# Root reciprocals spread by transposing broadcast columns, and two rescheduled norms of the mixer outputs, in a one-core fp32 encoder layer

## What is computed

```python
h = rms_norm(x, norm1_g) * (1 + sc1) + sh1         # norm 1, all 1024 positions
z = h @ w_in                                       # 19 units of 128 columns
ya, yb, yc, yd = gmlp(z), dsa(z), pool(z), swa(z)  # four mixers, 256 features each
y = _rms(stack([ya, yb, yc, yd])) * mix_out_g      # each mixer's 256 features by themselves
x = x + g1 * (y @ w_out)
h = rms_norm(x, norm2_g) * (1 + sc2) + sh2         # norm 2
x = x + g2 * conv_glu(h, w_up, conv, w_down)
out = rms_norm(x, final_g)                         # final norm
```

## Time and profile before

| | us |
|---|---|
| median of 3 runs | 1311.04 |
| the runs | 1307.82 to 1311.52 |
| the profiled execution, its own time | 1310.75 |
| its span, first to last instruction | 1309.0 |
| busy: PE, DVE, ACT, POOL | 1217.2, 718.3, 595.2, 630.1 |

### The profile page before, as it was taken

One profiled execution on the slowest core, in us unless ns is written; L12 is line 12 of the kernel. 1 busy time (PEld: TensorE's weight loads), 2 busy tenths in 40 slices (PEclk: granted clock), 3 DMA queues, 4 the chain that ended last, 5 costly groups with the idle time before them and its releaser, 6 DMA issues.

```text
span 1309.0 us, 16977 instructions
## 1 busy us (share of the span) xinstructions
PE 1217.2 (93%) x5618; PEld 995.1 (76%) x5618; DVE 718.3 (55%) x1404; ACT 595.2 (45%) x1007; POOL 630.1 (48%) x317
## 2 busy tenths in 40 slices
PE   3798999987899799999999999989799999999996
PEld 1686778866788588888878887878588888888874
DVE  6943877887857788889984444353522112211224
ACT  4236556654842455224422676542455224422442
POOL 1135576783304255445555566424255445544553
PEclk9999999987989799999999999999899999999998
DMA  8447753450112122242223443314222222222223
GB/s 311 147 178 261 203 171 110 146 165 17 49 65 96 50 97 97 94 133 97 97 95 130 132 137 128 130 57 139 76 98 97 93 99 95 99 94 95 97 100 128
DMA packets 58565, 153.87 MB, mean 118 GB/s; under 512 B 6504, under 2 KB 20200, under 8 KB 58512
## 3 DMA queue, kind: packets, MB, share of 16 engines
q1 hardware_dynamic: 47472, 135.12, 30.5%
q10 hardware_dynamic: 11040, 18.09, 4.2%
HBM read 142.66 MB, written 10.52 MB: 117 GB/s over the span
## 4 chain that ended last, share of the span: by engine, by line
PE 35%; issue 32%; POOL 16%; DVE 9%; DMA 3%; ACT 2%; ACTq 1%; POOLq 1%; SPq 0%; DVEq 0%
POOL w_lo L554 11%; PE ps L1779 8%; PE ps L1782 8%; PE ps L1780 8%; DVE unread L1282 4%; POOL act_lo L703 3%; PE ps L2058 2%; POOL w_ada L593 1%; PE ps L1760 1%; PE ps L1763 1%; PE ps L1761 1%; PE ps L2037 1%; PE ps L2047 1%; DMA w_ada<-in_w_ada 1%; DMA qi_dram<-qi_lo 1%
## 5 line engine op out<-in xcount | busy, mean ns | idle before, releaser
L554 POOL TENSOR_TENSOR w_lo<-w_raw,w_hi 128x1024 fp32r<-128x1024 f32 x152 | 364.6, 2399 | 487.5 <-ACT w_hi L715 487.5
L1779 PE MATMUL ps<-h_hi,w_hi 128*128 128x512 f32 x928 | 371.5, 400 | 11.6 <-DVE h_lo L1240 7.0
L1780 PE MATMUL ps<-h_lo,w_hi 128*128 128x512 f32 x928 | 364.3, 393 | 0.0
L1782 PE MATMUL ps<-h_hi,w_lo 128*128 128x512 f32 x928 | 345.6, 392 | 0.0
L715 ACT ACTIVATE w_hi<-w_raw 128x1024 fp32r<-128x1024 f32 x152 | 161.1, 1060 | 358.9 <-PE ps L1782 351.3
L1779 PEld LDWEIGHTS ps<-h_hi,w_hi 128*128 128x128 f32 x928 | 175.7, 189 | 56.7 <-DVE h_lo L1240 8.5
L1782 PEld LDWEIGHTS ps<-h_hi,w_lo 128*128 128x128 f32 x928 | 175.5, 189 | 37.6
L1780 PEld LDWEIGHTS ps<-h_lo,w_hi 128*128 128x128 f32 x928 | 176.3, 190 | 33.4
L1665 DVE SCALAR_TENSOR_TENSOR ps<-conv_in,conv_w,ps 128x512 f32<-128x512 f32 x44 | 33.2, 754 | 215.0 <-ACT ps L1090 215.0
L1779 PE MATMUL ps<-act_hi,w_hi 128*128 128x512 f32 x352 | 140.3, 398 | 5.0 <-POOL act_lo L703 2.6
L1782 PE MATMUL ps<-act_hi,w_lo 128*128 128x512 f32 x352 | 137.6, 391 | 0.0
(11 more groups left out here) (240 smaller groups left out, 1801.6 us busy)
## 6 DMA issues: line engine op xcount, KB each, us to landing
w_raw<-in_w SPq DMA_DIRECT2D x173, 512.0 KB, 3.3
w_ada<-in_w_ada SPq DMA_DIRECT2D x48, 512.0 KB, 4.2
x_sb<-in_x SPq DMA_DIRECT2D x4, 1024.0 KB, 9.9
q_st<-qk_dram SPq DMA_DIRECT2D x32, 128.0 KB, 4.1
out<-fin_o ACTq DMA_DIRECT2D x16, 256.0 KB, 2.1
qi_st<-qi_dram ACTq DMA_DIRECT2D x18, 128.0 KB, 3.6
qk_dram<-qk_hi ACTq DMA_DIRECT2D x4, 512.0 KB, 2.7
qk_dram<-qk_lo ACTq DMA_DIRECT2D x4, 512.0 KB, 3.7
```

Source lines behind the costliest of these rows:

```text
L554: pool.tensor_tensor(r(w_lo[:, slot]), w_raw[:, slot], w_hi[:, slot], ALU.subtract).then_inc(w_lo_ready, 1)
L1779: pe.matmul(ps[:, bank], r(hi_t[:, kk]), r(xh(kk)), start=(i == 0), stop=False)
L1780: pe.matmul(ps[:, bank], r(hi_t[:, kk]), r(xl(kk)), start=False, stop=False)
L1782: mm = pe.matmul(ps[:, bank], r(lo_t[:, kk]), r(xh(kk)), start=False, stop=last_k)
```

## The change

1. **Spread without diagonals.** `root` ends with the reciprocal. `spread` transposes, for each block, the column `root_r[:, t]` broadcast to 128 columns.
2. **gMLP squares on DVE.** In half 0 the four sums of squares of the gMLP rows are taken by DVE right behind `gmlp_output`; ACT no longer takes them. `y_roots` waits for them.
3. **Late squares one column up.** `late_squares(7)` and `y_roots` of half 1 move on ACT from k = 7 to k = 6, ahead of that step's `split_unit` and `square`.
4. **Late rows scaled in place.** In half 1 the rows of y are multiplied by their factor in SBUF, gMLP and pool on DVE (two instructions), SWA and DSA on ACT (eight), and PE transposes them; the diagonals of half 1 go.

```diff
-                squared = 16 * h
+                squared = 12 * h
...
+                def scale_late_rows(positions):
+
+                    act.wait_ge(y_inverted, 2)
+                    for m_ in positions:
+                        cols = slice(W * Y_GROUPS[m_], W * Y_GROUPS[m_] + W)
+                        for b in range(HB, NBLK):
+                            at_ = 4 * m_ + b - HB
+                            ins = act.activation(y[:, b, cols], y[:, b, cols], ACT.Copy, scale=y_scale[:, at_:at_ + 1])
+                        ins.then_inc(y_scaled_act, 1)
...
                         if k == NBLK + 1:
-                            y_roots(slice(0, 12), 15)
+                            act.wait_ge(gmlp_squared, HB)
+                            y_roots(slice(0, 12), 11)
...
                         if k == NBLK:
                             act.wait_ge(gmlp_out, 4)
-                            for b in range(HB):
-                                y_squares(b, (0,), junk)
                             act.wait_ge(swa_biased, NBLK)
...
+                            if k == 6:
+                                late_squares(NBLK - 1)
+                                y_roots(slice(0, 16), 28)
                             if k == 7:
-                                late_squares(NBLK - 1)
-                                y_roots(slice(0, 16), 32)
+                                scale_late_rows((2, 3))
                             split_unit(nd + k + 2)
...
-            def root(m, diag, blocks=HB):
+            def root(m, blocks=HB):
 
                 dve.wait_ge(root_ready, m + 1)
-                vlink(dve.reciprocal(root_r[:, 0:blocks], root_s[:, 0:blocks]))
-                dve.tensor_tensor(diag.rearrange("p (t c) -> p t c", c=P),
-                                  ident[:].unsqueeze(1).to_broadcast([P, blocks, P]),
-                                  root_r[:, 0:blocks].unsqueeze(2).to_broadcast([P, blocks, P]),
-                                  ALU.mult).then_inc(diag_ready, 1)
+                dve.reciprocal(root_r[:, 0:blocks], root_s[:, 0:blocks]).then_inc(root_inverted, 1)
...
+                def scale_late_rows(positions):
+                    dve.wait_ge(y_root_ready, 3)
+                    dve.reciprocal(y_scale[:], y_root[:]).then_inc(y_inverted, 2)
+                    dve.wait_ge(y_inverted, 2)
+                    for m_ in positions:
+                        rows = y[:, HB:NBLK, W * Y_GROUPS[m_]:W * Y_GROUPS[m_] + W]
+                        dve.tensor_tensor(rows, rows, y_scale[:, 4 * m_:4 * m_ + 4].unsqueeze(2).to_broadcast([P, HB, W]),
+                                          ALU.mult).then_inc(y_scaled, 1)
+
+                def gmlp_squares():
+                    dve.wait_ge(gmlp_out, 4)
+                    for b in range(HB):
+                        dve.scalar_tensor_tensor(out=gmlp_junk[:, b], in0=y[:, b, 0:W], scalar=1.0, in1=y[:, b, 0:W],
+                                                 op0=ALU.mult, op1=ALU.mult, accum_out=y_sum[:, b:b + 1]
+                                                 ).then_inc(gmlp_squared, 1)
...
                             for g in range(4):
                                 gmlp_output(g)
+                            gmlp_squares()
...
                         if k == 6:
-                            y_scales(1, range(4), 3)
+                            scale_late_rows((0, 1))
...
-            def spread(m, bank, diag, blocks=HB):
-
-                pe.wait_ge(diag_ready, m + 1)
-                for i in range(blocks // HB):
-                    mm = pe.matmul(ps[:, bank + i], ones[:], diag[:, HALF * i:HALF * i + HALF], start=True, stop=True)
-                mm.then_inc(rms_spread, 1)
+            def spread(m, bank, blocks=HB):
+
+                pe.wait_ge(root_inverted, m + 1)
+                for t in range(blocks):
+                    tr = pe.transpose(ps[:, bank + t // HB, P * (t % HB):P * (t % HB) + P],
+                                      root_r[:, t:t + 1].to_broadcast([P, P]), ident[:])
+                tr.then_inc(rms_spread, 1)
...
-                    pe.wait_ge(y_diag_ready, 4 * h + i // 2 + 1)
+                    if h == 0:
+                        pe.wait_ge(y_diag_ready, i // 2 + 1)
+                    elif i < 4:
+                        pe.wait_ge(y_scaled, i // 2 + 1)
+                    else:
+                        pe.wait_ge(y_scaled_act, i // 2 - 1)
...
-                        tr = pe.matmul(ps[:, Y_BANKS[h][i], P * t:P * t + P], y[:, HB * h + t, P * g:P * g + P],
-                                       diag_y_of[h][:, i // 2, t], start=True, stop=True)
+                        at_, rows = ps[:, Y_BANKS[h][i], P * t:P * t + P], y[:, HB * h + t, P * g:P * g + P]
+                        if h == 0:
+                            tr = pe.matmul(at_, rows, diag_y[:, i // 2, t], start=True, stop=True)
+                        else:
+                            tr = pe.transpose(at_, rows, ident[:])
```

More of the change, by code:

```diff
@@ L127, in build @@
         rms_x = at("rms_x", [P, S], RB + 12288)
-        diag_x = at("diag_x", [P, S], RB + 16384)
         h_t = at("h_t", [P, 2, S], RB)
@@ L155, in build @@
         p_t = at("p_t", [P, 2, HB, P], RE + 4096)
-        diag_y_of = [at("diag_y_0", [P, 4, HB, P], RB + 4096), at("diag_y_1", [P, 4, HB, P], RE)]
+        diag_y = at("diag_y", [P, 4, HB, P], RB + 4096)
+        gmlp_junk = at("gmlp_junk", [P, HB, W], RB + 12288)
         sum2 = at("sum2", [P, HALF], RB + 28672)
-        diag2 = at("diag2", [P, HALF], RB + 30720)
         onehot = at("onehot", [32, S + P], RG)
@@ L270, in build @@
         root_ready = sem("root_ready")
-        diag_ready = sem("diag_ready")
+        root_inverted = sem("root_inverted")
         rms_spread = sem("rms_spread")
@@ L345, in build @@
         y_diag_ready = sem("y_diag_ready")
+        y_inverted = sem("y_inverted")
+        y_scaled = sem("y_scaled")
+        y_scaled_act = sem("y_scaled_act")
+        gmlp_squared = sem("gmlp_squared")
         x2_loaded = sem("x2_loaded")
@@ L1042, in _ @@
                     dsa_squares(HB - 1)
-                    y_roots(slice(12, 16), 16)
+                    y_roots(slice(12, 16), 12)
                 n0, s0 = N1 + 16 * h, 2 * KD + 16 * h
@@ L1210, in _ @@
             ada_tile(0, 1)
-            root(0, diag_x[:], NBLK)
+            root(0, NBLK)
             ada_tile(1, 0)
@@ L1557, in early_out, with y_scales @@
                                       ALU.mult).then_inc(dsa_out_ready, 1)
-                def y_scales(hh, groups, roots):
+                def y_scales(groups, roots):
                     dve.wait_ge(y_root_ready, roots)
@@ L1563, in y_scales @@
                     for m_ in groups:
-                        dve.tensor_tensor(diag_y_of[hh][:, m_], ident[:].unsqueeze(1).to_broadcast([P, HB, P]),
+                        dve.tensor_tensor(diag_y[:, m_], ident[:].unsqueeze(1).to_broadcast([P, HB, P]),
                                           y_scale[:, 4 * m_:4 * m_ + 4].unsqueeze(2).to_broadcast([P, HB, P]),
                                           ALU.mult).then_inc(y_diag_ready, 1)
+                def scale_late_rows(positions):
[12 more added lines that the diff above has]
+                                                 ).then_inc(gmlp_squared, 1)
                 if h == 0:
@@ L1600, in _ @@
                                 gmlp_output(g)
+                            gmlp_squares()
                         if k == NBLK + 1:
-                            y_scales(0, range(3), 1)
-                    y_scales(0, range(3, 4), 2)
+                            y_scales(range(3), 1)
+                    y_scales(range(3, 4), 2)
                 n0, s0 = N1 + 16 * h, 2 * KD + 16 * h
@@ L1645, in _ @@
                 else:
-                    root(2, diag2[:])
+                    root(2)
                     vlink(dve.memset(sum2[:], 0.0))
@@ L1652, in _ @@
                         final_norm(0, g)
-                root(1 + 2 * h, diag2[:])
+                root(1 + 2 * h)
                 dve.wait_ge(rms_spread, 2 + 2 * h)
@@ L1708, in _ @@
                         if k == 6:
-                            y_scales(1, range(4), 3)
-            root(4, diag2[:])
+                            scale_late_rows((0, 1))
+            root(4)
             dve.wait_ge(rms_spread, 5)
@@ L1722, in _, with over_features @@
             pe.sem_inc(residual_added, 2)
-            def over_features(m, count, bank, sums, diag, blocks=HB):
+            def over_features(m, count, bank, sums, blocks=HB):
                 row_sums(count, bank, sums, blocks)
-                spread(m, bank, diag, blocks)
+                spread(m, bank, blocks)
             def row_sums(count, bank, sums, blocks=HB):
@@ L1747, in _ @@
             last.then_inc(bias_row_made, 1)
-            over_features(0, KD, 4, sum_x, diag_x, NBLK)
+            over_features(0, KD, 4, sum_x, NBLK)
             pe.wait_ge(bias_row_out, 1)
@@ L2022, in _ @@
```

(6 more changed lines are left out.)

## The result

The changed kernel took 1292.2 us (median of 4 runs, 1288.57 to 1293.01) beside 1309.43 for the kernel before (4 runs): a ratio of 0.9866, 95% interval 0.9835 to 0.9897. Measured twice more it was 0.9865 (0.9843 to 0.9887) and 0.9858 (0.9834 to 0.9883). The mean of the three, 0.9863, is 17.9 us. The forecast was 15.9 us and 1295.0. The direction, the places and most prices held. The gain was 1.3 us larger than forecast in the first measurement and 2 us over all three; most of the 2 us lie in one term, the turning of y in half 1. The time itself came out 2.8 us under 1295. Of these 1.3 us are the larger gain, and 1.3 us are the base, which the forecast took as 1310.75 and which was 1309.43 here.

A forecast was written before the change was run, and what follows sets the result against it. PE, busy 1217 of 1309 us, was taken as the bound, with gains only where it waits or runs at 1.2 GHz. 5.1 + 0.4 + 0.9 + 5.4 + 4.1 = 15.9 us off 1310.75 gives 1294.9, stated as 1295; range 1292 to 1302.

The forecast's parts named there:

- Norm 2 and last norm: Norm 2 of both halves and the last norm: PE starts sooner with four transposes, 1.7 us each, 5.1 for three.
- Slow broadcast columns: Rival for the norms: broadcast columns load slowly, so only the diagonals' time is won; 1298.2 us, chance 0.05.
- m = 2: Final norm of half 0, beside the first w_out unit: only PE's time counts, 0.4 us, bounds 0 and 0.5.
- Norm 1: First norm (m = 0): without the diagonal h_t starts sooner, limited by POOL's subtractions; 0.9 us, bounds 0 and 3.0.
- POOL is not in the way: Rival in norm 1: POOL does not hold DVE back, 2.1 us more gained, 1292.8 us; chance 0.07.
- Turning of half 0: Turning of y, half 0: passes start 3.4 us sooner, full clock saves 2.4, less 0.4 for delays: 5.4 us.
- clock falls all the same: Rival in the turning of y, half 0: PE's clock still drops, since its work there is small; 1297.4 us, chance 0.12.
- the early gain doesn't reach the end: Rival: the 5.4 us from half 0 is lost because the load of x or DVE's key search keeps pace; 1300.3, chance 0.08.
- Turning of half 1: Turning of y, half 1: earlier root and four transposes instead of eight passes start w_out 4.1 us sooner; bounds 1.0 and 5.0.
- The rule that speaks against this: Half 1's turning: the skill says transposes do not engage the full clock; then it is worth 1.0 us, time 1298.
- Clock stays down: Rival in half 1: the clock stays low behind the late transposes, w_out at 869.9, gain 1.0 us, 1298; chance 0.18.
- slower: Rival after half 1's turning: clock stays at 1.2 GHz deep into w_out, up to 38 us lost, 1333; chance 0.03.

## Why the prediction was right in most terms, and the step that failed

- **Norm 2 and last norm, 5.1.** Right: 1.68, 1.68 and 1.7 to 1.9. A column read 128 times loads like a stored one: four transposes took 1.11 us against 1.09 in the earlier trace rows, both at a granted clock of 0.50. *Slow broadcast columns* is refuted.
- **m = 2, 0.4.** Right, 0.3 to 0.4.
- **Norm 1, 0.9; measured 1.3 to h_t and 1.2 to PE.** The step "the product starts ahead of POOL, and POOL waits for it" was drawn right; POOL's two then took 4.80 us from 27.41, ending at 32.2 and not 32.5, and the reciprocal to h_t shrank accordingly. The prediction misreads one row on the way: of POOL's two subtractions in the earlier trace rows the first ended at 30.02 and the second at 33.30, so the product of 27.72 did not end with either, but 1.1 us behind the first; only the one-element sum ended with one. The sum does not hang on it. The rival that POOL is not in the way is refuted: both small operations stood behind it, and the run with the product moved shows the wait going to h_t. The Trainium skill ("SBUF — State Buffer", Who interferes with whom) states that a DVE instruction with two inputs in SBUF contends with a GpSimd instruction that reads SBUF, and that the ports they share are an exclusive lock; the rows agree: in the changed kernel the two small operations ended at 29.93 and 32.23, POOL's subtractions at 29.91 and 32.21.
- **Turning of half 0, 5.4; measured 5.7.** Counted from the gMLP output, copy, root, last copy and first pass came within 0.2 us of the forecast's times, the passes in 7.12 us. The passes start 3.6 us sooner (forecast 3.4) and are 2.1 us shorter up to w_out (9.25 to 7.12 us, forecast 2.4), and the 0.4 taken off for small delays was not lost. The squares on DVE ended 1.4 us ahead of the root, covered as said. The granted clock was 1.00 from 360 to 400 us in all ten traces of kernels with this part; *clock falls all the same* is refuted. That *the early gain doesn't reach the end* is refuted: this part alone gave 7.2 us, and 403.3 to 403.5 us follow in either kernel; what deviates from it does so without this part too (405.4 with the late part alone, 401.7 with the spreads alone).
- **Turning of half 1, 4.1; measured 4.6, 5.7 and 5.7. This is the step that failed.** The order of events was right: against the unit's end, column 7 ended at 3.5 us (forecast 3.8), tile 4 began at 5.8 (5.9). But the forecast wrote "I take the clock as down at 864", a certainty made from the one trace with diagonals. In the first trace it did fall, at 855.1, 0.6 us behind the start of tile 4 (w_out at 10.2, forecast 10.7). In the two others it stayed up: w_out at 9.05, a gain of 5.7, which is 0.7 beyond the upper bound of 5.0 that the forecast gave for that very case. With it up, tiles 4 to 7 take 2.60 us and not 3.45, and the whole stretch is 1.2 us shorter, where the forecast had 0.9. The mean of the three traces is 5.3, so this term was 1.2 us too small; norm 1 and half 0 add 0.4 and 0.3, and together that is the 2 us.
- **The rule that speaks against this.** The rule of the Trainium skill ("TensorE: Matmul & The Clock Gate", Part 4: PE-mode transpose) does not hold in this stretch: the clock was at 1.00 when the 32 transposes began and stayed there in six of nine traces. In the first trace of the changed kernel it even came back, at 858.6, where PE had done nothing since 854.5 but transposes and, from 857.7, row sums. *Clock stays down* and *slower* are refuted with it.
- **What was not priced at all** is where the clock falls in the input projection, in the attention stage and between 424 and 849 us. No bias of it shows in the whole change, but it moves a run by 2 us and more, and the difference of two traces by 4. The same page of the Trainium skill (Part 1: The HAM clock gate) says of the start of a kernel that the number of matmuls at the lower clock differs between runs of one and the same kernel. The traces show the like in the middle of a kernel: the attention stage at 0.91 or 0.83.

**What stays open.** The terms account for the whole change and for the late part, alone and in company. The intervals are 2 to 3 us wide either way. The terms do not account for the spreads (9.8 and 11.3 us alone, 5.5 in company, 7.2 in the stretches) nor the squares (7.2 alone, 3.0 in company, 5.7 in the stretch). Alone they sum to 17 us and more; both together, without the late part, gave 12.7 (1 - 0.9903). In the runs' mean granted clock the share lost is visible: 0.971 before, 0.977 with spreads alone (0.978 the second time), 0.977 with squares alone, 0.978 with all; at two times the missing share of the span that is 77, 60, 59 and 57 us at 1.2 GHz. That reads as if either of the two took away nearly as much of the lower clock as both together, so that they share some 5 us. But it is not shown: the kernel with the spreads and the late part, without the squares, has a mean of 0.975 over its six runs, which is less than the spreads alone have. Which stretch this sits in was not found: single traces differ by as much.

## What to carry to other kernels

Where a norm's factor goes through DVE, PE and back, transposing the broadcast column takes one link out of the chain, and the forecast from four rows of the old trace was right to 0.2 us each time in the changed kernel (1.7 to 1.9 for 1.7). Where DVE works beside GpSimd, moving one operation ahead only handed the wait to the next; what shortened the stage here was to fill DVE's idle time until the product behind h_t, too, was out of GpSimd's way. And before one reads a few us out of two traces, a second trace of the same kernel tells which stretches stand still and which move by themselves.

## What the runs showed of the hardware

TensorE's clock fell at different places in executions of one program: the changed kernel's attention at 0.91 or 0.83, 62.8 to 67.2 us. In the late turning it stayed at 2.4 GHz in six of the nine traces with transposes, and fell in all seven with the diagonals. POOL's pair of subtractions took 4.64 to 6.12 us for the same work: 4.64 and 4.80 where no product of DVE ran between the two, 5.97 and 6.12 where one of 1024 elements with two operands in SBUF did.
